# Running the heads of a gated recurrence in pairs, with GpSimd updating the decays, in a decoder step on one core

## What is computed

```python
def step(S, chunk):
    qc, kc, gc, vc = chunk
    b = jnp.cumsum(gc, axis=2)
    diff = jnp.where(causal, b[:, :, :, None, :] - b[:, :, None, :, :], -jnp.inf)
    att = jnp.einsum('bhtk,bhsk,bhtsk->bhts', qc, kc, jnp.exp(diff))
    out = jnp.einsum('bhtk,bhkv->bhtv', qc * jnp.exp(b), S) + jnp.einsum('bhts,bhsv->bhtv', att, vc)
    b_last = b[:, :, -1:, :]
    S = jnp.exp(b_last[:, :, 0, :])[..., None] * S + jnp.einsum('bhsk,bhsv->bhkv', kc * jnp.exp(b_last - b), vc)
    return S, out
```

## Time and profile before

| | |
|---|---|
| median of three runs | 1977.64 us (1977.2 to 1979.1) |
| profiled execution, its own time | 1976.55 us |
| its span | 1974.6 us |
| TensorE busy | 1724.5 us, 87% |
| VectorE busy | 803.4 us, 41% |
| GpSimd busy | 542.7 us, 27% |
| ScalarE busy | 432.9 us, 22% |
| mean granted TensorE clock | 0.918 |

### The profile page before, as it was taken

The page is one execution under the profiler, slowest core; times in us unless marked ns, Lnnn a source line. Parts: engine busy times, 40 slices in busy tenths (PEclk is TensorE's granted clock), DMA queues, the critical chain, the costliest instruction groups (busy, mean ns, idle before and its releaser), DMA issues.

```text
span 1974.6 us, 28840 instructions
## 1 busy us (share of the span) xinstructions
PE 1724.5 (87%) x12863; PEld 1577.7 (80%) x12863; DVE 803.4 (41%) x1160; ACT 432.9 (22%) x576; POOL 542.7 (27%) x202
## 2 busy tenths in 40 slices
PE   2899999998797799877599978776688899999997
PEld 1799999998765799866388755554687899999997
DVE  4412111135217599866576654221465412111121
ACT  2311111112133123200123333221122211111111
POOL 0233343334312123300011122332122233333331
PEclk9999999999688899966599989887799999999999
DMA  4132233223311122201132137887512122333222
GB/s 136 43 86 73 74 101 86 79 69 117 121 48 34 55 89 86 75 23 44 51 115 67 68 126 284 316 303 299 207 64 86 49 80 73 89 90 82 79 74 78
DMA packets 191499, 203.43 MB, mean 103 GB/s; under 512 B 7104, under 2 KB 176832, under 8 KB 182928
## 3 DMA queue, kind: packets, MB, share of 16 engines
q1 hardware_dynamic: 172336, 105.56, 18.7%
q0 software_dynamic: 11680, 75.57, 10.5%
q10 hardware_dynamic: 7360, 20.47, 2.7%
HBM read 187.21 MB, written 14.30 MB: 102 GB/s over the span
## 4 chain that ended last, share of the span: by engine, by line
PE 75%; DVE 12%; DMA 6%; ACT 3%; issue 3%; SPq 0%; POOL 0%; ACTq 0%; DVEq 0%
PE ps L1291 21%; PE ps L1292 20%; PE ps L1293 20%; DMA k_page<-in_cache_k,kv_row 3%; DMA v_page<-in_cache_v,kv_row 2%; PE ps L1638 2%; PE ps L1591 1%; PE ps L1609 1%; DVE att L1033 1%; PE ps L1714 1%; DVE m_hi L1233 1%; DVE nf L841 1%; DVE n_lo L844 1%; ACT n_hi L515 1%; PE ps L1653 1%
## 5 line engine op out<-in xcount | busy, mean ns | idle before, releaser
L411 POOL TENSOR_TENSOR w_lo<-raw,w_hi 128x2048 fp32r<-128x2048 f32 (+1 forms) x108 | 456.7, 4229 | 1071.9 <-ACT w_hi L500 1071.9
L1291 PE MATMUL ps<-n_lo,w_hi 128*128 128x288 f32 x1856 | 557.6, 300 | 26.7 <-DVE n_lo L844 17.5
L1292 PE MATMUL ps<-n_hi,w_lo 128*128 128x288 f32 x1856 | 551.1, 297 | 0.0
L1293 PE MATMUL ps<-n_hi,w_hi 128*128 128x288 f32 x1856 | 549.3, 296 | 0.0
L1291 PEld LDWEIGHTS ps<-n_lo,w_hi 128*128 128x128 f32 x1856 | 351.6, 189 | 44.6 <-issue 28.7
L1293 PEld LDWEIGHTS ps<-n_hi,w_hi 128*128 128x128 f32 x1856 | 352.9, 190 | 0.0
L1292 PEld LDWEIGHTS ps<-n_hi,w_lo 128*128 128x128 f32 x1856 | 352.1, 190 | 0.0
L500 ACT ACTIVATE w_hi<-raw 128x2048 fp32r<-128x2048 f32 (+1 forms) x108 | 187.9, 1740 | 287.9 <-PE ps L1293 279.6
L856 DVE TENSOR_TENSOR hf<-sg,ps 128x576 f32<-128x576 f32 x44 | 33.2, 754 | 449.6 <-ACT sg L526 449.6
L1292 PE MATMUL ps<-hid_hi,w_lo 128*128 128x288 f32 x704 | 207.7, 295 | 0.0
L1293 PE MATMUL ps<-hid_hi,w_hi 128*128 128x288 f32 x704 | 207.5, 295 | 0.0
(11 more groups left out here) (256 smaller groups left out, 2317.1 us busy)
## 6 DMA issues: line engine op xcount, KB each, us to landing
raw<-in_w_in SPq DMA_DIRECT2D x23, 1024.0 KB, 5.3
raw<-in_ffn_w_gate SPq DMA_DIRECT2D x44, 512.0 KB, 4.0
raw<-in_ffn_w_up SPq DMA_DIRECT2D x44, 512.0 KB, 5.3
raw<-in_ffn_w_down SPq DMA_DIRECT2D x32, 704.0 KB, 4.5
scratch_g<-g_out ACTq DMA_DIRECT2D x8, 576.0 KB, 2.8
gates<-scratch_g ACTq DMA_DIRECT2D x4, 1152.0 KB, 8.8
raw<-in_w_out SPq DMA_DIRECT2D x4, 1024.0 KB, 4.9
scratch_x<-xT ACTq DMA_DIRECT2D x1, 2304.0 KB, 12.6
```

Of the source, the lines that this page charges most:

```text
L411: pool.tensor_tensor(w_lo[:, u % NRAW, :n], raw[:, u % NRAW, :n], w_hi[:, u % NW, :n].bitcast(F32), ALU.subtract).then_inc(S("w_lo_done"), 1)
L1291: pe.matmul(dst, hi, x_lo, start=first, stop=False)
L1292: pe.matmul(dst, lo, x_hi, start=False, stop=False)
L1293: return pe.matmul(dst, hi, x_hi, start=False, stop=last)
```

## The change

The heads run as pairs: h = 2g + a, with a = 0, 1 taking turns within each level. `left`, att, att_s, k_rows, state, state_s and v_own exist twice. q_lev and k_lev no longer alternate by level but belong to a head each, and so do the PSUM banks 4 and 5 (and 6 and 7). The updates of left and decay move from VectorE to GpSimd, with two semaphores a head: level_in tells GpSimd that the factors of a level are made, decayed that an update is finished. TensorE's level L of a head now waits for the masked copy of level L - 1 of that head. After the levels the two heads' state chains follow each other, outputs in banks 0 and 4, and the sample states of both are added at the end of the pair. On GpSimd's queue, two state loads stand before the decays of pair 0, two stores between the pairs, and two loads between levels 2 and 3 of pair 1.

```diff
+        def level_views(h, L):
+            b = LEVELS[L]
+            dec, lft = level_view(decay[:, h, :], L), level_view(left[:, h % 2, :], L)
+            right = dec[:, :, 1, :]
+            n = right.shape[1]
+            return (dec[:, :, 1, b - 1:b].to_broadcast([P, n, b]), dec[:, :, 0, b - 1:b].to_broadcast([P, n, b]),
+                    lft[:, :, 0, :], right)
...
+            def decays(g):
+                for L in range(1, len(LEVELS)):
+                    for a in range(2):
+                        b = LEVELS[L]
+                        end, mid, first, right = level_views(2 * g + a, L)
+                        pool.wait_ge(S(f"level_in{a}"), 8 * g + L)
+                        if L > 1:
+                            pool.wait_ge(S(f"decayed{a}"), 2 * (7 * g + L - 1))
+                        pool.tensor_tensor(first, first, end, ALU.mult).then_inc(S(f"decayed{a}"), 1)
+                        pool.wait_ge(S(f"decayed{a}"), 2 * (7 * g + L - 1) + 1)
+                        pool.tensor_tensor(right, right, mid, ALU.mult).then_inc(S(f"decayed{a}"), 1)
+                    if g and L == 2:
+                        state_load(2)
+                        state_load(3)
...
-                    dve.wait_ge(S("level_in"), 8 * h + L)
-                    link(dve.tensor_tensor(view(left[:, :])[:, :, 0, :], view(left[:, :])[:, :, 0, :], end, ALU.mult))
-                    link(dve.tensor_tensor(right, right, mid, ALU.mult))
-                    level_out(L - 1)
...
+                for L in range(1, len(LEVELS)):
+                    for a in range(2):
+                        h = 2 * g + a
+                        if L > 1:
+                            dve.wait_ge(S(f"level_done{a}"), 8 * g + L)
+                        if L > 1:
+                            dve.wait_ge(S(f"decayed{a}"), 2 * (7 * g + L - 1))
...
+                            dve.tensor_tensor(into_k[:, :, 0, :], k[:, :, 0, :], level_view(left[:, a, :], L)[:, :, 0, :],
+                                              ALU.mult).then_inc(S(f"level_in{a}"), 1)
+                        level_out(a, L - 1)
...
-                    if L:
-                        pe.wait_ge(S("level_in"), 8 * h + L)
-                    if L >= 2:
-                        pe.wait_ge(S("level_out"), 8 * h + L - 1)
...
+                        if L:
+                            pe.wait_ge(S(f"level_in{a}"), 8 * g + L)
+                            pe.wait_ge(S(f"level_out{a}"), 8 * g + L)
...
+                    pe.wait_ge(S("v_own_done"), h + 1)
+                    pe.wait_ge(S("k_rows_done"), 2 * g + 2)
+                    if a:
+                        pe.wait_ge(S("state_done"), 4 * h + 4)
```

More of the change, by code:

```diff
@@ L785, in _ @@
             split(at_unit["feat", 5] + 2)
-            for h in range(HB):
-                head(h)
-            act.wait_ge(S("state_out"), 16 * HB)
+            for g in range(2):
+                heads(g)
+            for m in range(2):
+                act.wait_ge(S(f"state_out{m}"), 32)
             output_norm()
@@ new lines, in heads @@
+                for a in range(2):
+                    h = 2 * g + a
+                    dve.wait_ge(S("o_summed"), h + 1)
+                    link(dve.tensor_tensor(state_s[:, a, :, :], state_s[:, a, :, :],
+                                           decay[:, h, NQ - 1:NS:NQ].unsqueeze(2).to_broadcast([P, NB, VD]), ALU.mult))
+                    dve.wait_ge(S("head_read"), h + 1)
+                    for m in range(2):
+                        part = state_s[:, a, 4 * m:4 * m + 4, :]
+                        ins = dve.tensor_tensor(part, part, ps[:, 2 + m if a else 5 + 2 * m, :].rearrange("p (b v) -> p b v", b=4),
+                                                ALU.add)
+                    ins.then_inc(S("state_s_done"), 1)
```

268 lines of the change are left out of this document (137 added, 131 removed).

## The result

The changed kernel took **1954.23 us** (median of 4 runs, 1943.64 to 1958.05), the kernel before, on the same chip, 1978.37 (4 runs, 1977.2 to 1980.81). The profiled execution of the changed kernel took 1958.05 us, its span 1956.2, at a mean granted TensorE clock of 0.930 (0.918 before).

What follows compares the result with a forecast made beforehand. No engine is full, so a dependent chain through the four heads' recurrence was taken as the bound. Gains of 5.3 (pair 0) and 6.5 (pair 1) less 0.6 and 0.9 make 10.3, from 1977.64 to 1967.3 us; 8-in-10 range 1956 to 1985.

Steps and rivals of the forecast that it cites:

- levels from level 2 with last step, pair 0: First two heads: levels 2 to 7 take 27.2 us, the last step 4.85.
- levels with last step, pair 1: Last two heads: level 2's decay ends at 9.6 us, levels 3 to 7 22.4, loads +1.2, last step 4.85.
- chains, pairs 0 and 1: State chains of two heads, one directly after the other: 9.96 + 9.9 us in pair 0, 12.9 + 10.0 in pair 1.
- turns: Between levels and state chains: only the second head's transposes remain, 1.4 us a pair, k_rows of the first being out.
- tails: End of each pair, after its second chain, where VectorE adds the sample states: 1.3 us.
- allowances of 0.6 and 0.9: Taken off the gain: 0.6 us for TensorE at low clock in levels 2 and 3, 0.9 for v_own and store issue.
- The round of two heads: One level of both heads: GpSimd's products plus VectorE's q and k summed on the shared port, 4.8 us, later 4.4.
- a higher clock in the second chain: Second state chain of a pair at a higher TensorE clock: worth up to 2.9 us, 12.9 against 10.0.
- A: GpSimd's small strided products in the rounds cost more, 1.2 us instead of 0.82: time 1986, slower; chance 0.22.
- B: VectorE is woken before GpSimd's next product: rounds 5.0 to 5.4 us, later 4.7 to 5.1; time 1970 to 1975; chance 0.23.
- D: No overlap: TensorE at low clock through all rounds, 5.0 us each, only turns saved; time 1972 to 1977; chance 0.05.
- C: Short products do not exclude each other on the port, or it interleaves: rounds shorter, time 1954 to 1960; chance 0.10.

Runs made afterwards that it cites:

- e4: Changed kernel with VectorE's q and k products taking one input from PSUM from level 2 on, attention entries not computed: 1934.54 us, ratio 0.9821.
- e11: Changed kernel with one more GpSimd product, by ones, after each decay update (six a round instead of four): 1961.74 us, ratio 0.9948.
- e2: Changed kernel, heads still in pairs, but left and decay products kept on VectorE: 1955.23 us, ratio 0.9905.
- e3: Kernel before, heads one at a time, with left and decay products moved from VectorE to GpSimd: 1985.03 us, ratio 1.0069.
- e7: Changed kernel with state loads moved behind levels 4 and 5 and v_own made in level 1: 1948.93 us, ratio 0.9887.
- e8: e7 plus ScalarE copying both keys and one query of a pair to PSUM for VectorE, full computation: 1941.0 us, ratio 0.9842.
- e5: Kernel before, unaltered, run and profiled again: 1971.06 us, ratio 0.9998.
- e12: e8 with one more 128-column identity matmul on TensorE behind each level product: 1936.57 us, ratio 0.9828.
- e6: Changed kernel with 27 dummy VectorE products ahead of the output norm, delaying everything behind the heads: 1980.46 us, ratio 1.0031.
- e10: Kernel before with two more 128-column identity matmuls on TensorE behind each product of levels 1 to 7: 1966.68 us, ratio 0.9974.
- e9: Changed kernel with one more 128-column identity matmul on TensorE behind each product of levels 1 to 7: 1951.4 us, ratio 0.9897.
- e1: Changed kernel, unaltered, run and profiled again: 1951.98 us, ratio 0.9907.

## Why the prediction was wrong in its size

Direction and the mechanism of the port held; the gain was more than twice the forecast, because the products in the rounds were priced too high and the chains at too low a clock. The recurrence, from the start of the span to the last state addition, ends at 937.14, where my steps led to 951.7 (888 + 63.7) before loose ends, and the kernel before ended at 963.52. So 14.6 us are to be explained, term by term on the first profile:

| term | forecast | measured | off by |
|---|---|---|---|
| levels from level 2 with last step, pair 0 | 32.05 | 28.7 | -3.4 |
| levels with last step, pair 1 | 38.05 | 35.25 | -2.8 |
| chains, pairs 0 and 1 | 19.9 + 22.9 | 16.2 + 19.7 | -6.9 |
| turns | 1.4 + 1.4 | 0.7 + 1.2 | -0.9 |
| start of level 2 in pair 0 | 833.5 | 832.5 | -1.0 |
| tails | 1.3 + 1.3 | 1.5 + 1.4 | +0.3 |

The allowances of 0.6 and 0.9 that I took off besides were not needed.

**The round of two heads** (first step that failed). I had it right that it is a sum on the port: e4 takes the port away and a round falls from 3.55 to 2.71, e11 adds 0.68 of GpSimd and it rises by twice 0.34. The durations were too large. GpSimd's undisturbed product of 256 columns takes 0.62 to 0.67 (forecast 0.76), of 288 columns 0.67 for decay and 0.79 to 0.94 for left (forecast 0.82). My line through 544 and 2048 columns lies 0.14 too high at 256 columns; four products came out 0.56 too long. And the port changes hands better than I counted: VectorE's q passes between left and decay and costs about 0.08, only k stops GpSimd, 0.36. I had expected q to be stretched, to 1.2; from level 4 on it was mostly k, to 0.86. Hence 3.55 in the rounds shown and 3.7 in the mean of the eight, instead of 4.4 in levels 4 to 7. With 288 columns pair 0's two rounds took 5.34 and 4.50, against 4.8 each, as forecast in their sum. The 2.6 cycles an element that the Trainium skill states (GPSIMD Engine Reference, Elementwise — side-by-side cycle accounting) gave, as an estimate, 0.62 for 288 columns and 0.55 for 256; measured are 0.67 (decay) and 0.62, nearer to it than my line, but left took 0.79 and more. The same page's advice to keep elementwise work on VectorE (Engine selection) is not borne out by the heads here: e2 follows it and its heads are 7.9 us longer, while the medians do not tell the two apart. In e3, with nothing to interleave, the levels gain nothing by leaving VectorE.

**The chains** (second step). I took "9.96 + 9.9" and "12.9 + 10.0", rows of the kernel before, as if a chain had one duration. It follows the clock: 6.87 where it stays high (e4, e7 and e8 have such rows), 9.96 to 10.1 at a mean of 0.67, 12.9 at 0.50. The changed kernel's four took 36.0 to 36.1 us in all, in both its profiles. I had named "a higher clock in the second chain" and let it "stretch the range a little", at up to 2.9, without a term in the sum; the chains came out 6.9 shorter than forecast. Against e5, where head 2 took 10.0, they gained 39.85 - 36.0 = 3.9, against the first profile 6.7; that difference is most of the 3.2 between the two gains of the heads.

**Pair 0 and pair 1.** The first products of GpSimd came at 830.74 (forecast 831.7). The first level of pair 1 took 7.05 (forecast 6.2); its state loads in the queue (1.82 at 891.44) and the second chain's start were as described.

**The rivals.** A (dear small products) is refuted by the rows: 0.82 against VectorE's 0.46 was my estimate against a row, and measured are 0.62 against 0.41 for 256 columns. B (VectorE first) is refuted by the rounds, 3.4 to 4.1 where it had 4.7 to 5.1, and D by the clock, 0.82 in the heads. C's number, 1954 to 1960, fits the time, but by luck: its mechanism does not hold, the port is exclusive (e4). By my estimate now, the same sum with 0.62 for GpSimd's products and chains of 8 to 9 would have come out near the measured time.

**The sample attention** (not in my sum). It takes 221 to 236 us in profiles of these kernels with the same instructions, and most of the 6 to 14 us between runs of one kernel may come from it: the two profiles of the changed kernel differ by 14.8 us in time and by 13.7 there. Medians less the profile's start of that stage give a tail of 810 to 811 for the changed kernel, 806 to 810 for the one before; so 26.6 become 24 in the first comparison and 23.4 become 19 in the second. Whether that is a cost of the change or chance stays open: by the same count the other kernels have 805 to 813 us (e12, whose profile is not near its median, 796), and e6, with the same heads but a later start, 808.

What also stays open is what sets the clock in a chain. e10 raised it with more TensorE work in the levels, in e9 and e12 it was lower with more work, and e4, e7 and e11, which do not touch TensorE's work, had it higher in some chains than e1.

## What to carry to other kernels

When two engines share a port, price a loop as a sum over the port and look for a second independent chain first: pairing brought two thirds of the gain in the heads here, and the move to the slower engine paid only inside it. Never carry a duration of a dependent chain of matmuls over without the clock it ran at: the same chain took 6.9 to 12.9 us. For the same reason, count such chains apart when you read an experiment: in e7 and e12 they, and not the edit's own mechanism, made the difference in the heads. And put one input of the short product that blocks the other engine into PSUM if it can be had there.

## What the hardware showed that I had not expected

- GpSimd's product on strided views is no dearer than the contiguous rows of 544 and 2048 columns lead one to estimate (0.76 for 256 columns): 0.62 to 0.67 us for 256 columns in blocks of 8 to 64, 0.67 for 288 in blocks of 1 to 4 (decay). The product for left takes 0.79 to 0.94 in the small blocks; its views are strided and broadcast like those of decay, and why it is dearer stays open.
- The port is handed over between two products of GpSimd that stand 0.07 us apart in the records: VectorE's q at 849.69 got in between left (until 849.89) and decay (from 849.96), which took 0.70 instead of 0.63.
- Two more 128-column matmuls behind each level went with a higher granted clock in the heads of the kernel before (0.71 to 0.83, 4.7 us), one more with slower chains in the changed one (36.0 to 40.2 us) and in e12 (29.4 to 38.2).
